# Gate rows of the expert blocks: one transfer of two blocks in place of one for each block

## The reference

```
def one_chunk(args):
    xc, ec, gc = args                       # tokens, the 8 x 16 experts picked per token, their gates
    u = expert_u[ec]
    a = jax.nn.gelu(jnp.einsum('cd,chkd->chk', xc, u))
    return jnp.einsum('chk,chkd->cd', gc * a, expert_v[ec])
```

## Time and profile before

| | us |
|---|---|
| median of three runs | 1865.88 |
| lowest and highest | 1864.47, 1874.83 |
| the profiled execution | 1874.42 |
| its span (first to last instruction) | 1872.7 |
| busy: PE, DVE, POOL, ACT | 1626.6, 1309.1, 742.3, 574.7 |
| mean granted TensorE clock | 0.932 |

### The profile page before, as it was taken

How to read it: one execution, slowest core, us unless ns; L and a number is a source line. 1 busy time by engine, 2 the same in 40 slices (tenths; PEclk the granted TensorE clock), 3 DMA queues, 4 the chain that set the end, 5 groups by cost and what they waited for, 6 DMA issues and landing times.

```text
span 1872.7 us, 24792 instructions
## 1 busy us (share of the span) xinstructions
PE 1626.6 (87%) x7621; PEld 1256.3 (67%) x7621; DVE 1309.1 (70%) x2645; ACT 574.7 (31%) x983; POOL 742.3 (40%) x694
## 2 busy tenths in 40 slices
PE   7899999999784544857599999999999999999996
PEld 2444444444554443747498888888888898889885
DVE  0624321312389996963789989898988889898988
ACT  1110032301211264433233333333333333333332
POOL 1000100000100187852366556565647555656553
PEclk9899999999897755988799999999999999999998
DMA  9854211114000000679899999999999999999994
GB/s 364 304 212 147 101 45 45 45 45 183 1 1 1 6 12 1 179 203 299 325 376 376 356 375 350 386 351 373 348 369 371 350 364 372 377 351 385 353 376 146
DMA packets 192961, 450.59 MB, mean 241 GB/s; under 512 B 30355, under 2 KB 79763, under 8 KB 192540
## 3 DMA queue, kind: packets, MB, share of 16 engines
q1 hardware_dynamic: 136732, 245.47, 36.5%
q0 software_dynamic: 56192, 204.66, 28.1%
HBM read 426.65 MB, written 23.36 MB: 240 GB/s over the span
## 4 chain that ended last, share of the span: by engine, by line
PE 29%; DVE 19%; POOL 17%; issue 17%; DMA 14%; ACT 1%; SPq 1%; POOLq 0%; DVEq 0%; ACTq 0%
PE bank L683 21%; POOL v_rows L582 9%; DMA v_rows<-v_exp,small 9%; DVE acc L1578 6%; POOL hot L606 5%; DMA w_scratch<-staged 3%; PE bank L805 3%; DVE acc_x L1578 2%; DVE v_lo L1527 2%; DMA ada_blk<-ada_w 2%; POOL small L648 2%; DVE u_lo L1521 1%; DVE u_rows L1551 1%; PE bank L768 1%; PE bank L843 1%
## 5 line engine op out<-in xcount | busy, mean ns | idle before, releaser
L869 PE MATMUL bank<-h_hi,u_hi 128*128 128x320 f32 x1024 | 316.8, 309 | 14.9 <-DVE u_lo L1521 14.9
L870 PE MATMUL bank<-h_lo,u_hi 128*128 128x320 f32 x1024 | 317.2, 310 | 0.0
L871 PE MATMUL bank<-h_hi,u_lo 128*128 128x320 f32 x1024 | 317.0, 310 | 0.0
L582 POOL DMA_INDIRECT v_rows<-v_exp,small x192 | 281.0, 1464 | 84.2 <-issue 49.6
L582 POOL DMA_INDIRECT u_rows<-u_exp,small x192 | 223.6, 1165 | 110.1 <-issue 48.8
L869 PEld LDWEIGHTS bank<-h_hi,u_hi 128*128 128x128 f32 x1024 | 193.0, 189 | 20.2 <-issue 15.1
L892 PE MATMUL bank<-v_hi,g_both 128*128 128x512 f32 x512 | 206.5, 403 | 0.0
L890 PE MATMUL bank<-v_hi,g_both 128*128 128x512 f32 x512 | 206.1, 403 | 0.0
L891 PE MATMUL bank<-v_lo,g_both 128*128 128x512 f32 x512 | 205.6, 402 | 0.0
L683 PE MATMUL bank<-ring,hT 128*128 128x512 f32 x448 | 197.8, 598 | 0.8 <-ACT zv L986 0.8
L870 PEld LDWEIGHTS bank<-h_lo,u_hi 128*128 128x128 f32 x1024 | 193.0, 188 | 6.4
(11 more groups left out here) (212 smaller groups left out, 2552.4 us busy)
## 6 DMA issues: line engine op xcount, KB each, us to landing
u_raw<-u_by_key SPq DMA_DIRECT2D x128, 512.0 KB, 6.0
v_raw<-v_exp SPq DMA_DIRECT2D x128, 512.0 KB
w_row<-w_scratch SPq DMA_DIRECT2D x128, 160.0 KB
ada_blk<-ada_w SPq DMA_DIRECT2D x9, 2048.0 KB, 18.6
ring<-w_in SPq DMA_DIRECT2D x9, 2048.0 KB, 8.5
w_scratch<-staged SPq DMA_DIRECT2D x2, 8192.0 KB, 30.6
ring<-ada_w SPq DMA_DIRECT2D x3, 2048.0 KB, 12.6
xr<-x SPq DMA_DIRECT2D x8, 512.0 KB, 11.7
```

Source lines behind the costliest of these rows:

```text
L582: pool.indirect_dma_start(out=rows[:, s], out_offset=None, in_=table, in_offset=bass.IndirectOffsetOnAxis(ap=ix[:, s:s + 1], axis=0))\
L869: pe.matmul(o, u_hi[:, r, k], h2_hi[:, k], start=(k == 0), stop=False)
L870: pe.matmul(o, u_hi[:, r, k], h2_lo[:, k], start=False, stop=False)
L871: last = pe.matmul(o, u_lo[:, r, k], h2_hi[:, k], start=False, stop=(k == KD - 1))
```

## The change

The gates of two blocks are loaded in one transfer. `load_gates` takes a pair of slots (0 and 1, or 2 and 3) and reads the gates of blocks b and b + 1, which lie side by side in `w_scratch`: 320 KB, 2.5 KB for each partition. The refills with q = 1 and q = 3 issue it, those with q = 0 and q = 2 load no gates. The two slots of a pair share a semaphore. The four loads ahead of the first block become two.

```
-            def load_gates(q, b):
-                sp.dma_start(w_row[:, q], w_rows[b]).then_inc(w_row_in[q], 16)
+            def load_gates(pair, b):
+                two = slice(b, b + 2) if isinstance(b, int) else bass.ds(b, 2)
+                sp.dma_start(w_row[:, 2 * pair:2 * pair + 2], w_dram[:, two]).then_inc(w_row_in[pair], 16)
...
-            for q in range(STEP):
-                load_gates(q, q)
+            for pair in range(STEP // 2):
+                load_gates(pair, 2 * pair)
...
                 load_experts(q, b + STEP)
-                load_gates(q, b + STEP)
+                if q % 2:
+                    load_gates(q // 2, b + STEP - 1)
...
-                dve.wait_ge(w_row_in[q], 16 * turn(b, q))
+                dve.wait_ge(w_row_in[q // 2], 16 * turn(b, q))
```

## The result

The changed kernel takes 1881.61 us (median, 1874.37 to 1887.88) against 1866.45 us before (1855.44 to 1880.62), 20 runs each. The ratio is 1.0073, with a 95% interval of 1.0049 to 1.0096: slower by about 13.6 us. From the median of the forecast, 1865.88 us, that ratio leads to 1879.5 us. This is just inside the stated range of 1853 to 1881 us, but it isn't the "no change" of the forecast of 1870 us; what came is the size and the side of the rival "slower", which had 1878 us.

A forecast was written before the change was run, and what follows sets the result against it. Bound: a per-step ring through the gather of v, 30.55 us. Terms +0.38 - 0.25 = +0.13 us a step, 31 times, +4.0 us on 1865.9 gave 1870 us, called no change; range 1853 to 1881 us.

The forecast's parts named there:

- rival "slower": Refill 1's doubled load holds v's rows, refill 0 gives nothing back: 1878 us, up to 1889; chance 0.19.
- signs of being wrong: L648's mean distance moves over 0.3 us, DVE waits for gates at L1534 in the loop, or u's rows late at L1551.
- What bounds the kernel: Each step's round from POOL's index copy through v's landing to DVE's last adds: 30.55 us, claimed for all 31 uses.
- v ring: POOL gathers v, rows land, DVE adds, POOL may issue again; the forecast's only ring, 30.55 us a step.
- u ring: POOL gathers u, rows land, DVE takes dot products, POOL may issue again; forecast put changes around this gather at nothing.
- Prices of pieces: Engine time per DMA piece, 10 ns plus 0.037 ns a byte: 57 ns at 1.25 KB, 105 ns at 2.5 KB.
- The total of 0.16 us less a step: Engine time saved by fewer gate pieces, useful only ahead of v's landing; as a rival 1861 us, chance 0.14.
- Refill 0 (and 2) without gates, -0.25 us: Gates gone ahead of v's gather save 0.25 us a step, bounds nothing to 0.92; gates gone before u's gather: nothing.
- Refill 1 (and 3) doubled, +0.38 us, at most 0.76: Two blocks' gates among v's rows cost 0.38 us a step, bounds nothing to 0.76; refill 3's growth costs nothing.
- One for one: SP's and POOL's pieces alternate singly while both queues have work, so longer pieces delay rows; sum the same 4 us.
- Fixed costs: Rival: each gate load holds up its block by 2.28 us, so 64 fewer save 146 us: 1720 us; chance 0.01.
- rule on whole packets in turn: Engines alternate between rings by packets of some 9 to 17 descriptors; the forecast sum would be the same 4 us.

The follow-up runs named there:

- no_gates: Kernel before without the 124 gate loads after the first four (outputs not the reference's): 1867.25 us, ratio 0.9976 to before.
- pair_0_2: Changed kernel with its joined gate loads issued in refills q = 2 and q = 0 instead of 1 and 3: 1859.30 us, ratio 0.9907 to the kernel before.
- two_at_0_2: Changed kernel with two blocks' gates loaded at q = 0 and 2, in two transfers with 1.25 KB pieces: 1859.22 us, ratio 0.9947 to the kernel before.
- pair_3_only: Kernel before with only the gates of slots 2 and 3 joined, in refill 3; slots 0 and 1 load singly: 1883.48 us, ratio 1.0061 to before.
- two_at_1_3: Changed kernel, same refills, each joined load split into two transfers with 1.25 KB pieces: 1871.46 us, ratio 0.9985 to the kernel before.
- uv_halves: Kernel before with u and v loaded in pieces of 2 KB instead of 4 KB: 1855.78 us, ratio 0.9895 to before.
- gates_first: Changed kernel with the gates issued ahead of u and v in the refill: 1890.60 us, ratio 1.0116 to the kernel before.
- pair_2_3: Changed kernel with the joined gate loads in refills 2 and 3 instead of 1 and 3: 1867.70 us, ratio 0.9999 to the kernel before.
- uv_halves_0_2: Kernel before with u and v in 2 KB pieces and two blocks' gates at q = 0 and 2 in 1.25 KB pieces: 1869.66 us, ratio 0.9966 to before.

## Why the prediction was right and wrong

The measured time lies inside the range, and that is luck: no term of the sum was borne out. One of the prediction's own signs of being wrong came: the rows of u are late at L1551 (L1553 of the changed kernel) in every step. Another was just missed: the mean distance of the copies ahead of the gathers of v (L648, now L650, 911.2 to 1836.3 us) is 30.84 us, 0.28 more than before, where 0.13 was forecast and 0.3 was the sign.

- **What bounds the kernel**: right that it is a ring through a gather that lands late, and that TensorE and the DMA share only look like the bound. Wrong that it is one ring. I read one step of one execution, where the v ring ran, and said "31 times over". The first four steps of that very trace were in the u ring (here the waits that the view puts down to the gather of u, 900 to 1030 us), and another execution spends half its steps there. That was the step that failed first: the changed kernel is slow in the u ring, which my text had set aside, since at 1159.97 every piece of that gather "has long passed".

```profile
DVE u_rows L1551 <- DMA u_rows<-u_exp,small: 11.0, 3, 5.7
```

- **Prices of pieces**: 57 and 105 ns went into terms that the runs refuted as terms. The total of 0.16 us less a step gave no gain, and taking away all 1.82 us gave nothing that can be told (no_gates).
- **Refill 0 (and 2) without gates, -0.25 us**: not found. The kernels that load two blocks' gates there are faster than the kernel before (pair_0_2, two_at_0_2).
- **Refill 1 (and 3) doubled, +0.38 us, at most 0.76**: the sign was right, but the term was put on refill 1 and the rows of v, and refill 3 was put at nothing. In the u ring a step grew by 30.82 - 29.75 = 1.07 us, and it did so with refill 3 alone (pair_3_only, from 950 us on (1824.9 - 961.3) / 28 = 30.84). The bytes by themselves didn't make it, since the same bytes in short pieces at the same place cost 0.2 us a step (29.94, from five steps only).
- **One for one**: the reading that a longer piece is a longer turn, which the rows beside it wait for, is the only one of mine that gave the side of two_at_1_3 and uv_halves at once. Its sizes were too large each time, and gates_first, pair_2_3 and uv_halves_0_2 went otherwise than I wrote. Its premise fell too: in uv_halves SP began 531 pieces beside 294 of POOL. So the cause is known as far as this: joined pieces at the refills 1 and 3 cost about 0.9% over short pieces at the same place, and joined pieces at 0 and 2 cost nothing that can be told. By which mechanism is open.
- **The time**, worked out afterwards from two traces of the kernel before: a step 1.07 us longer against a kernel that is in the u ring for 4 to 15 of 31 steps, and 0.17 longer against its v ring (30.82 against 30.65) in the others, is 9 to 19 us (4 x 1.07 + 27 x 0.17, 15 x 1.07 + 16 x 0.17). Measured are 13.6.
- **Fixed costs** of a transfer: 64 transfers fewer brought nothing, as the rows said: pair_0_2 and two_at_0_2 differ by these 64 and have medians of 1859.30 and 1859.22 us. The fixed 2.0 us of the Trainium skill (DMA: Bandwidth & Descriptors, Anatomy of one DMA) is fitted there to transfers issued from GpSimd, and these loads are issued by SP, blocks ahead; no such cost is seen. Its rule on whole packets in turn (Queues, rings and completion order) is left undecided: no trace here shows where a packet ends, and two_at_1_3 has two loads where the changed kernel has one, so their packets may differ too.
- **Chances**: 0.20 stood on slower, 0.49 on the forecast. The slower rival's number, 1878 us, came near by luck. Its mechanism didn't come: it had the bytes of refill 1 hold the rows of v, and pair_3_only, with refill 1 as before, has the same long u ring, while two_at_1_3 has the same bytes and isn't slow.

## What to carry to other kernels

Before a price is multiplied by the number of steps, look at the waits of several stretches and of a second execution: a loop with two gathers can have two rings, and the same code may run in either. Where loads of one queue run beside a gather that somebody waits for, joining small pieces into longer ones can slow the gather, here by 0.9%; try the joined load ahead of the awaited rows (0.9907), or the big loads cut finer (0.9895). Busy DMA engines are no proof that bytes are the bound: leave the bytes out once, and see.

## What the hardware showed that I had not expected

- 124 loads of 160 KB taken from DMA engines that are 95% busy changed the time by a ratio of 0.9976 (0.9948 to 1.0005), that is by nothing that can be told.
- 1 MB a block in pieces of 2 KB in place of 4 KB was faster by 1.05%, with 36,864 pieces more (229,825 against 192,961).
- While both queues had work, each had about half of the engines' time (46.4 to 53.6%), whether SP began 270 or 531 pieces in 5 us.
- One program has executions from 1855 to 1881 us with all clocks alike. In the two that were traced it slips from a ring of 29.75 us to one of 30.65 us, after four steps in the one and after about fifteen in the other.
